# A gated linear recurrent unit moved from 128-row tiles to one 96-row weight block per tile, with its result brought back to 128 rows by DMA inside SBUF

## The chip, the core and the metric

The program runs on one core of one Trainium2 chip. The metric is the device time of one execution in microseconds (us); lower is better. The program before was timed three times: 2656.78, 2657.13 and 2657.72 us, median 2657.13 us. Engines are named as in the profile: PE (TensorE matmul), PEld (its weight load), DVE (VectorE), ACT (ScalarE), POOL (GpSimd), SP (SyncE, which here only issues the loads of the big weights).

## What is computed

Two transformer blocks run one after the other on one sequence of 256 tokens, width 2048, all in float32. The first block (gated linear attention, latent attention, SwiGLU) is not touched. The second block has two layers; each projects the normed input onto ten parts and mixes them by retention, differential attention and a linear recurrent unit of width 768. The change is in that last one, whose gates are block diagonal: 8 blocks of 96 columns.

```python
LRU_W, LRU_BLOCKS, LRU_BW = 768, 8, 96
def rg_lru(x, conv_w, conv_b, wa, ba, wx, bx, lam):
    xc = conv_b + xp[:, 0:S] * conv_w[0]          # causal convolution, 4 taps
    for j in range(1, CONV_W):
        xc = xc + xp[:, j:j + S] * conv_w[j]
    xb = xc.reshape(B, S, 8, 96)
    r = sigmoid(einsum('bsnk,nkj->bsnj', xb, wa) + ba)
    i = sigmoid(einsum('bsnk,nkj->bsnj', xb, wx) + bx)
    log_a = 8 * r * log_sigmoid(lam); a = exp(log_a)
    b = sqrt(-expm1(2 * log_a)) * (i * xc)
    h = scan over tokens of  h_t = a_t * h_(t-1) + b_t
lru_out = rg_lru(lx, ...) * silu(lg)              # part of the layer's mixed vector
y = concatenate([ret_out, diff_out, lru_out]) @ w_out
```

## The kernel before

**Units.** Every big product is a job, cut into units of 512 KB of weights. A unit's weights are loaded by SP into one of five `raw` slots. ACT rounds them into `whi` (the part that a fast float32r matmul takes exactly), DVE subtracts to get the rest, `wlo`, and PE multiplies: twelve matmuls of 512 columns a unit (or of 384 for the jobs `lx` and `lg`). `whi` and `wlo` have four slots. The order is fixed by `make_timeline`: before each unit n stands the preparation of unit n+3, and after each unit one step of each stage that is under way, such as the recurrent unit. All five engines run through that one list, each taking its own share and waiting on semaphores. So a stage's ACT and DVE work stands in the same queues as `whi` and `wlo`.

**Jobs around the recurrent unit.** In each layer of the second block the jobs are `rvg 0`, `lx 0`, `lx 1`, `rvg 1`, `dq`, `dk`, `dv`, `dg`, three `rqk`, `rvg 2`, `lg 0`, `lg 1` and four `w2`, each of eight units. The texts below call the units of `dq` dq1 to dq8 and those of `dk` dk1 to dk8. When `rvg 1` is done ACT evacuates it (`rv`, then `rg` with silu, which needs a table load before and leaves one behind).

**The recurrent unit, per layer and half (`hb` 0, 1).** PE transposes the projected columns into a PSUM bank per 128 rows (three banks `tp`, `lx_T`), ACT copies them to `LXT`. DVE runs the convolution, one `tensor_scalar` and three `scalar_tensor_tensor` per 128-row tile, a tile per step (`lx_conv`). The gates (`lru_g`, first for r, then for i) are plain float32 matmuls `tp<-xc,wa`: since 96 does not divide 128, a 128-row tile of the result needs the blocks of two or three tiles of the input, in all seven matmuls of 256 columns over three banks for 384 columns of a gate; the weights `WA` stand in 14 tiles of 128x128 which POOL first clears and then fills by 20 small DMAs (`ls_rn`). ACT applies the sigmoid per tile (`lxt<-tp,gcol`, `li<-tp,gcol`). `lru_a`: ACT exp and tanh per tile (`la<-lxt`, `lxt<-lxt`), DVE three elementwise operations over the half (768 columns). `lru_b`: ACT square root over the half (`xc<-xc`), DVE one product and a `tensor_tensor_scan` per tile. `lg_T`, some 200 us later, multiplies with silu of the gate and writes the tiles of `MXH` and `MXL`, the stationary operands of the last product.

The profile's `L825` is every matmul, `L828` every transpose, `L1260` every ACT function, `L1883`, `L1886`, `L1889` DVE's tensor_tensor, tensor_scalar and scalar_tensor_tensor, `L2331` the scan, `L2657` the DMAs of `WA`. The four TP banks are handed out in rotation, and a stage that writes a bank waits until its last reader is done (`empty`).

Of the kernel before, what the change touches and what calls it, by code (L numbers as in the profile page):

```python
# [16 lines left out]
P = 128  # L17
S = 256
# [119 lines left out]
NR1 = 94  # L138
R_CW, R_CB, R_BA, R_BX, R_LAM = 0, 48, 60, 72, 84
R_AB = 96  # L140
NR2 = 128
NRAW, NW = 5, 4
# [11 lines left out]
def lru_pieces():  # L154
    pieces, pairs = [], []
    for n in range(4):
        a0, a1 = 96 * n, 96 * n + 96
        cuts = [(max(a0, P * m), min(a1, P * m + P), m) for m in range(3) if max(a0, P * m) < min(a1, P * m + P)]
        for r0, r1, kt in cuts:
            for c0, c1, mt in cuts:  # L160
                if (kt, mt) not in pairs:
                    pairs.append((kt, mt))
                pieces.append((n, r0 - a0, r1 - a0, c0 - a0, c1 - a0, r0 - P * kt, c0 - P * mt, (kt, mt)))
    pairs.sort(key=lambda x: (x[1], x[0]))
    return pieces, pairs


PIECES, PAIRS = lru_pieces()
# [135 lines left out]
def stage_steps(sid):  # L304
# [64 lines left out]
    if kind == "lx":  # L369
        l, half = args  # L370
        return [idle, step(("lx_T", (l, half), 3))] + [step(("lx_conv", (l, 3 * half + m), 0)) for m in range(3)]
    if kind == "lru":
        (l,) = args
        return [x for hb in range(2) for x in (step(("lru_g", (l, hb, 0), 3)), step(("lru_g", (l, hb, 1), 3)), idle, step(("lru_a", (l, hb), 0)),
                                               step(("lru_b", (l, hb), 0)))]
# [194 lines left out]
def program(nc, ctx, I, CST, LVL, MSK, out):  # L570
# [3 lines left out]
    def sems(name, n):  # L574
# [11 lines left out]
    d_rowl, d_xr, d_gfb, d_gp, d_out = sem("d_rowl"), sems("d_xr", 2), sem("d_gfb"), sem("d_gp"), sem("d_out")  # L586

# [20 lines left out]
    lx_pad, xc_done, lru_exp, lru_tanh, lru_sum, lru_sqrt, scan_done, wa_zero = (  # L608
        sem(n) for n in ("lx_pad", "xc_done", "lru_exp", "lru_tanh", "lru_sum", "lru_sqrt", "scan_done", "wa_zero"))
# [46 lines left out]
    gcol = take("gcol", [224])  # L656
    modc = take("modc", [4, KD])
    cact = take("cact", [3, KD])
    clam = take("clam", [3, 12])
# [83 lines left out]
    LXT, XC, LA, LI = w2("lxt", 32, [6, 260]), w2("xc", 38.25, [6, S]), w2("la", 44.25, [3, S]), w2("li", 47.25, [3, S])  # L743
    DQT, DKT, DV, DG = w2("dqt", 32, [4, S]), [w2("dkt0", 44.25, [4, S]), w2("dkt1", 36, [2, S])], w2("dv", 48.25, [2, 512]), w2("dg", 52.25, [2, 512])
    WA = w2("wa", 56.25, [2, 14, P])
    RQK = w2("rqk", 56.25, [12, S])
    RAT = [w2("rat0", 68.25, [384]), w2("rat1", 90.25, [384])]
    DSX, DPT = [w2(f"dsx{i}", 91.75 + 1.5 * i, [384]) for i in range(2)], w2("dpt", 94.75, [384])
    RV, RG = w2("rv", 70.25, [2, 768]), w2("rg", 76.25, [2, 768])
    ST2 = [w2(f"st2{i}", 82.25 + 4 * i, [2, 512]) for i in range(2)]  # L750
# [70 lines left out]
    def pe_program(e):  # L821
# [38 lines left out]
        def rows(us):  # L860
            (u,) = us
            w.wait_ge(d_first, at("first"))
            bk = empty(u)
            tr(bk[:, 0:NR1], rows1[0:NR1, :], NR1)
            tr(bk[:, 128:128 + NR2], rows2[0:NR2, :], NR2).then_inc(tp_full[u.b], 1)

# [194 lines left out]
        def lx_T(us, l, half):  # L1061
            job = job_of["lx", l, half]
            w.wait_ge(gp_act[job["no"] % 2], at("gpa", *job["name"]))
            for m, u in enumerate(us):
                bk = empty(u)
                quad(bk, lambda a, t: ST2[job["st2"]][:, t, m * P:(m + 1) * P], 1).then_inc(tp_full[u.b], 1)

# [7 lines left out]
        def lru_g(us, l, hb, which):  # L1075
            m0 = 3 * hb
            w.wait_ge(wa_zero, l + 1)
            w.wait_ge(d_wa, 32 * len(PIECES) * (l + 1))
            for m in range(3):
                w.wait_ge(xc_done, at("xc", l, m0 + m))  # L1080
# [170 lines left out]
    def act_program(e):  # L1251
# [34 lines left out]
        def first_loads():  # L1286
            e.dma_start(cst[:, P:], CST[:, P:]).then_inc(d_first, 16)

            def rows(dst, r0, ap, n):
                e.dma_start(dst[r0:r0 + n, :], ap.rearrange("(r p) -> r p", p=P)).then_inc(d_first, 16)  # L1290
# [9 lines left out]
            rows(rows2, R_CW, I["lru_conv_w_2"].rearrange("l j d -> (l j d)"), 48)  # L1300
            rows(rows2, R_CB, I["lru_conv_b_2"].rearrange("l d -> (l d)"), 12)
            rows(rows2, R_BA, I["lru_ba_2"].rearrange("l d -> (l d)"), 12)
            rows(rows2, R_BX, I["lru_bx_2"].rearrange("l d -> (l d)"), 12)
            rows(rows2, R_LAM, I["lru_lambda_2"].rearrange("l d -> (l d)"), 12)
            rows(rows2, R_AB, I["ada_b"][0, 0:2 * D], 32)
# [19 lines left out]
        def rows(us):  # L1325
# [3 lines left out]
            copy(gcol[:, NR1:NR1 + NR2], bk[:, 128:128 + NR2]).then_inc(tp_act[u.b], 1)  # L1329
# [71 lines left out]
        def t_cexp(us):  # L1401
            gains()
            fn(clam[:, 0, :], gr(R_LAM, 12), ACT.Abs).then_inc(act_self, 1)
            w.wait_ge(act_self, own())
            fn(clam[:, 0, :], clam[:, 0, :], ACT.Exp, scale=-1.0).then_inc(act_self, 1)
            clam_exp[0] = own()

        def t_cln(us):
            w.wait_ge(act_self, clam_exp[0])
            fn(clam[:, 0, :], clam[:, 0, :], ACT.Ln, bias=unit_col).then_inc(clam_ln, 1)  # L1410
# [192 lines left out]
        def lx_T(us, l, half):  # L1603
            for m, u in enumerate(us):
                copy(LXT[:, 3 * half + m, 3:3 + S], full(u)[:, 0:S]).then_inc(tp_act[u.b], 1)
# [4 lines left out]
        def lru_g(us, l, hb, which):  # L1610
            m0 = 3 * hb
            gains()
            for m, u in enumerate(us):
                bk = full(u)
                dst = LXT[:, m0 + m, 0:S] if which == 0 else LI[:, m, :]
                if which == 1 and hb:
                    w.wait_ge(scan_done, at("scan", l, 0))
                fn(dst, bk[:, 0:S], ACT.Sigmoid, bias=gr((R_BX if which else R_BA) + 6 * l + m0 + m)).then_inc(tp_act[u.b], 1)
                note(tp_act[u.b], "tpa", *u)

        def lru_a(us, l, hb):
            m0 = 3 * hb
# [21 lines left out]
        def lg_T(us, l, half):  # L1644
            for m, u in enumerate(us):
                w.wait_ge(tp_dve[u.b], at("tpd", *u))
                copy(MXH[:, 10 + 3 * half + m, :], XC[:, 3 * half + m, :]).then_inc(mxg_hi, 1)
# [62 lines left out]
        def evac(us, no):  # L1710
# [167 lines left out]
    def dve_program(e):  # L1878
# [71 lines left out]
        def ada_mod(us, seq):  # L1950
# [4 lines left out]
            stt(scale, bk[:, 4:8], 1.0, gr(R_AB + KD + 4 * seq, 4), ALU.add, ALU.add).then_inc(dve_self, 1)  # L1955
            v = own()
            tt(shift, bk[:, 0:4], gr(R_AB + 4 * seq, 4), ALU.add).then_inc(tp_dve[u.b], 1)
# [80 lines left out]
        def t_cfin(us):  # L2038
            w.wait_ge(clam_ln, 1)
            gains()  # L2040
            stt(clam[:, 1, :], gr(R_LAM, 12), 0.0, clam[:, 0, :], ALU.min, ALU.subtract).then_inc(dve_self, 1)
            w.wait_ge(dve_self, own())
            ts(clam[:, 2, :], clam[:, 1, :], -8.0, None, ALU.mult).then_inc(clam_done, 1)
            ts(clam[:, 0, :], clam[:, 1, :], 8.0, None, ALU.mult).then_inc(clam_done, 1)
# [249 lines left out]
        def lx_T(us, l, half):  # L2294
# [452 lines left out]
```

## Time and profile before

| | |
|---|---|
| three timed runs | 2656.78, 2657.13, 2657.72 us (median 2657.13) |
| the profiled execution, span from the first to the last instruction | 2656.8 us |
| PE busy | 2569.4 us, 97% of the span |
| DVE, ACT, POOL busy | 1718.7 us (65%), 1303.5 us (49%), 76.9 us (3%) |
| mean granted TensorE clock | 0.996 |
| DMA traffic | 554.27 MB, mean 209 GB/s |

The page has no time of the profiled execution beyond its span, so the span is its own time here. A matmul in plain float32 stands in the trace as two records; the records are pipelined, so their single durations overlap and a group is read by its distance to the next. The view "chain" follows the work that ended last, piece by piece in order of time. The view "timeline" gives start, duration, engine, line, operation, tile and count, and in brackets the idle time before and what ended it.

### The profile page before, as it was taken

What the parts mean: (1) busy time and instruction counts of PE and PEld (TensorE: products, weight loads), DVE (VectorE), ACT (ScalarE), POOL (GpSimd) and SP (SyncE); (2) the same over time, 40 slices, a digit from 0 to 9 for tenths busy, and PEclk for the clock granted to TensorE, in tenths of its full rate; (3) what the DMA queues carried; (4) which work ended last, traced back from release to release, by engine and by line L of the source; (5) the groups of instructions that cost most, each with busy time, mean ns of one, the idle gap of its engine ahead of it and who ended that gap; (6) DMA issues with size and microseconds to landing.
All of it is one profiled execution on the core that took longest, in us unless ns stands there. A gap on an engine that the chain in (4) does not pass through costs nothing.

```text
span 2656.8 us, 35508 instructions
## 1 busy us (share of the span) xinstructions
PE 2569.4 (97%) x12983; PEld 2181.5 (82%) x12983; DVE 1718.7 (65%) x2262; ACT 1303.5 (49%) x1900; POOL 76.9 (3%) x116
## 2 busy tenths in 40 slices
PE   3989999999999999999999999999999999999999
PEld 3888887888887887888888888889888888888887
DVE  6877776776766756677655555566656655566664
ACT  3345455434555445444443444455654545565553
POOL 0000000000000000000000000002000101100000
PEclk9999999999999999999999999999999999999999
DMA  9975665887676765787666666566465465555564
GB/s 365 348 247 159 187 202 175 303 298 265 210 246 198 234 211 169 248 264 259 223 198 192 186 186 183 188 191 190 146 190 173 136 215 149 174 177 175 148 201 134
DMA packets 325063, 554.27 MB, mean 209 GB/s; under 512 B 24462, under 2 KB 135804, under 8 KB 324252
## 3 DMA queue, kind: packets, MB, share of 16 engines
q1 hardware_dynamic: 319104, 541.79, 64.1%
q0 software_dynamic: 3168, 7.12, 0.8%
q10 hardware_dynamic: 2620, 3.09, 0.3%
q8 instruction: 106, 1.74, 0.3%
q14 instruction: 65, 0.53, 0.1%
HBM read 549.83 MB, written 2.10 MB: 208 GB/s over the span
## 4 chain that ended last, share of the span: by engine, by line
PE 90%; DVE 4%; ACT 3%; issue 2%; DMA 1%; SPq 0%; POOL 0%; DVEq 0%; ACTq 0%
PE gp L825 82%; PE tp L825 5%; PE tp L828 2%; DMA raw_first<-in_ada_w_dram 1%; ACT whi L1260 1%; DVE wlo L1883 1%; DVE acc L1889 0%; ACT L1260 0%; DVE xs L1883 0%; ACT hraw L1260 0%; SPq L808 0%; DVE stat L2207 0%; ACT sx L1260 0%; DVE sx L1883 0%; DVE yd L1883 0%
## 5 line engine op out<-in xcount | busy, mean ns | idle before, releaser
L1883 DVE TENSOR_TENSOR wlo<-raw,whi 128x1024 fp32r<-128x1024 f32 (+1 forms) x830 | 983.2, 1197 | 641.0 <-ACT whi L1260 637.4
L1260 ACT ACTIVATE whi<-raw 128x1024 fp32r<-128x1024 f32 (+1 forms) x830 | 848.2, 1036 | 607.3 <-PE gp L825 483.6
L825 PE MATMUL gp<-whi,h 128*128 128x512 f32 (+1 forms) x2944 | 928.8, 387 | 6.1 <-DVE wlo L1883 4.6
L825 PEld LDWEIGHTS gp<-whi,h 128*128 128x128 f32 x2944 | 550.8, 188 | 107.6 <-issue 10.4
L825 PE MATMUL gp<-h,whi 128*128 128x512 f32 (+1 forms) x1936 | 605.5, 372 | 24.7 <-DVE wlo L1883 10.9
L825 PE MATMUL gp<-wlo,h 128*128 128x512 f32 (+1 forms) x1472 | 560.4, 381 | 0.0
L825 PE MATMUL gp<-h,wlo 128*128 128x256 f32 x1680 | 474.8, 283 | 0.0
L825 PEld LDWEIGHTS gp<-h,whi 128*128 128x128 f32 x1936 | 352.7, 192 | 96.4 <-issue 20.4
L825 PEld LDWEIGHTS gp<-h,wlo 128*128 128x128 f32 x1680 | 320.5, 191 | 0.8 <-issue 0.7
L825 PEld LDWEIGHTS gp<-wlo,h 128*128 128x128 f32 x1472 | 277.6, 189 | 45.2 <-issue 1.0
L1889 DVE SCALAR_TENSOR_TENSOR acc<-raw,cact,acc 128x1024 f32<-128x1024 f32 x149 | 190.5, 1278 | 7.4 <-DMA raw<-in_ada_w_dram 6.6
L825 PE MATMUL gp<-whi,ah 128*128 128x512 f32 x352 | 137.5, 391 | 0.0
L825 PE MATMUL gp<-whi,al 128*128 128x512 f32 x352 | 137.0, 389 | 0.0
L825 PE MATMUL gp<-wlo,ah 128*128 128x512 f32 x352 | 136.9, 389 | 0.0
L825 PE MATMUL gp<-whi,mxh 128*128 128x512 f32 x256 | 99.8, 390 | 0.0
L825 PE MATMUL gp<-whi,mxl 128*128 128x512 f32 x256 | 99.6, 389 | 0.0
L825 PE MATMUL gp<-wlo,mxh 128*128 128x512 f32 x256 | 99.6, 389 | 0.0
L825 PEld LDWEIGHTS gp<-whi,al 128*128 128x128 f32 x352 | 66.1, 188 | 13.9
L825 PEld LDWEIGHTS gp<-wlo,ah 128*128 128x128 f32 x352 | 66.1, 188 | 13.6
L825 PEld LDWEIGHTS gp<-whi,ah 128*128 128x128 f32 x352 | 66.1, 188 | 13.4
L2597 POOL TENSOR_TENSOR stat<-stat,cst 128x2 f32<-128x2 f32 (+1 forms) x37 | 30.1, 815 | 1467.6 <-DVE stat L1886 1467.5
L1260 ACT ACT_TABLE_LOAD x44 | 56.5, 1283 | 6.1 <-issue 2.8
(333 smaller groups left out, 2640.0 us busy)
## 6 DMA issues: line engine op xcount, KB each, us to landing
raw<-in_w_in_dram SPq DMA_DIRECT2D x310, 512.0 KB, 4.3
raw<-in_ffn_w_in_dram SPq DMA_DIRECT2D x176, 512.0 KB, 4.7
raw<-in_ada_w_dram SPq DMA_DIRECT2D x158, 512.0 KB, 5.0
raw<-in_w_out_dram SPq DMA_DIRECT2D x96, 512.0 KB, 4.3
raw<-in_ffn_w_down_dram SPq DMA_DIRECT2D x88, 512.0 KB, 4.3
raw<-in_w_in_dram SPq DMA_DIRECT2D x64, 384.0 KB, 3.5
raw_first<-in_ada_w_dram SPq DMA_DIRECT2D x34, 512.0 KB, 8.9
raw<-in_gla_wo_dram SPq DMA_DIRECT2D x32, 512.0 KB, 5.7
```

The costliest lines, as they stand in the source:

```text
L825: return e.matmul(o, l, r, start=start, stop=stop)
L828: return e.transpose(o, i, ident[0:n, 0:n])
L1260: return e.activation(o, i, f, **kw)
L1883: return e.tensor_tensor(o, a, b, op)
L1889: return e.scalar_tensor_tensor(out=o, in0=a, scalar=s, in1=b, op0=op0, op1=op1)
L2597: e.tensor_tensor(dst, dst, cst[:, C_HALF:C_HALF + n], ALU.pow).then_inc(pow_out, 1)
```

## The change

The recurrent unit works on 96 partitions, with one of the 8 weight blocks per tile. Per layer and half there are four tiles of 96 rows instead of three of 128.

- Transposes: eight of 96 columns into two banks instead of six of 128 into three. ACT copies two tiles of 96x2x256.
- Gates: four matmuls of a 96x96 block each instead of seven of 128x128, into two banks.
- Convolution, sigmoid, exp, tanh and scan run four times on 96 rows instead of three times on 128. The elementwise operations over a half have 1024 columns instead of 768.
- A half has one more convolution step, so the gates, `lru_a` and `lru_b` stand one unit later.
- `WA` is 96 rows by 8 blocks, filled by two DMAs a layer with no clearing.
- After the scan of each half POOL issues six DMAs from `XC` to `XG`, which has 128-row tiles. `lg_T`, the evacuation of `dg` and the rotation of `rqk` wait for them (`d_xg`).
- The small vectors are loaded in rows of 96, and the bias of the first block's modulation goes to the first of the two row tiles. Places in SBUF are dealt anew.

```diff
-PIECES, PAIRS = lru_pieces()
+    pieces = []
+    for b in range(4):
+        for m in range(3):
+            f0, f1 = max(BW * b, P * m), min(BW * b + BW, P * m + P)
+            if f0 < f1:
+                pieces.append((b, f0 - BW * b, f1 - BW * b, m, f0 - P * m))
...
-        return [idle, step(("lx_T", (l, half), 3))] + [step(("lx_conv", (l, 3 * half + m), 0)) for m in range(3)]
+        return [idle, step(("lx_T", (l, half), 2))] + [step(("lx_conv", (l, 4 * half + m), 0)) for m in range(4)]
...
     pe: lru_g
-            w.wait_ge(wa_zero, l + 1)
-            w.wait_ge(d_wa, 32 * len(PIECES) * (l + 1))
+            w.wait_ge(d_wa, 32 * (l + 1))
...
-                ks = [kt for kt, mt in PAIRS if mt == m]
-                for n, kt in enumerate(ks):
-                    last = mm(bk[:, 0:S], WA[:, which, 7 * hb + PAIRS.index((kt, m)), :], XC[:, m0 + kt, :], n == 0, n == len(ks) - 1)
+                for a in range(2):
+                    b = 4 * hb + 2 * m + a
+                    last = mm(bk[0:BW, a * S:(a + 1) * S], WA[0:BW, which, b, :], XC[0:BW, b, :], True, True)
...
     act: lru_a
-            for m in range(3):
-                ci = 6 * l + m0 + m
-                fn(LA[:, m, :], LXT[:, m0 + m, 0:S], ACT.Exp, scale=clam[:, 0, ci:ci + 1]).then_inc(lru_exp, 1)
+            for m in range(4):
+                ci = 8 * l + m0 + m
+                fn(LA[0:BW, m, :], LXT[0:BW, m0 + m, 0:S], ACT.Exp, scale=clam[0:BW, 0, ci:ci + 1]).then_inc(lru_exp, 1)
...
     act: evac
+                if kind == "dg":
+                    w.wait_ge(d_xg, 16 * len(PIECES) * (2 * args[0] + 2))
...
     dve: lru_b
-            for m in range(3):
-                e.tensor_tensor_scan(XC[:, 3 * hb + m, :], LA[:, m, :], LI[:, m, :], 0.0, ALU.mult, ALU.add).then_inc(scan_done, 1)
+            for m in range(4):
+                e.tensor_tensor_scan(XC[0:BW, 4 * hb + m, :], LA[0:BW, m, :], LI[0:BW, m, :], 0.0, ALU.mult, ALU.add).then_inc(scan_done, 1)
...
     dve: lg_T
-            w.wait_ge(scan_done, at("scan", l, half))
+            w.wait_ge(d_xg, 16 * len(PIECES) * (2 * l + half + 1))
...
     pool: ls_rn, lru_b
-            e.memset(WA[:, :, :, :], 0.0).then_inc(wa_zero, 1)
-            w.wait_ge(wa_zero, l + 1)
             for i, name in enumerate(("lru_wa_2", "lru_wx_2")):
-                for n, r0, r1, c0, c1, pr, pc, pair in PIECES:
-                    slot = PAIRS.index(pair)
-                    src = I[name][l, n:n + 5:4, r0:r1, c0:c1].rearrange("b r c -> r b c")
-                    e.dma_start(WA[pr:pr + r1 - r0, i, slot:slot + 8:7, pc:pc + c1 - c0], src).then_inc(d_wa, 16)
+                e.dma_start(WA[0:BW, i, :, :], I[name][l].rearrange("b r c -> r b c")).then_inc(d_wa, 16)
+
+        def lru_b(us, l, hb):
+            w.wait_ge(scan_done, at("scan", l, hb))
+            for b, r0, r1, m, p0 in PIECES:
+                e.dma_start(XG[p0:p0 + r1 - r0, 3 * hb + m, :], XC[r0:r1, 4 * hb + b, :]).then_inc(d_xg, 16)
```

ACT's queue in the first layer, from the gates of the first half to the exp and tanh of that half (`whi` is a unit's preparation, `rv` and `rg` the evacuation of `rvg 1`). Before:

```order
L1260 ACTIVATE lxt<-tp,gcol 128x256 x3
L1260 ACTIVATE whi<-raw 128x1024
L1260 ACTIVATE li<-tp,gcol 128x256 x3
L1260 ACTIVATE whi<-raw 128x1024 x2
L1260 ACTIVATE rv<-gp,stat 128x256 x2
L1260 ACT_TABLE_LOAD
L1260 ACTIVATE rg<-gp,stat 128x256 x2
L1260 ACT_TABLE_LOAD
L1260 ACTIVATE la<-lxt,clam 128x256 x3
L1260 ACTIVATE lxt<-lxt,clam 128x256 x3
```

The same place on ACT in the changed program:

```order
L1261 ACTIVATE lxt<-tp,gcol 96x256 x4
L1261 ACTIVATE whi<-raw 128x1024
L1261 ACTIVATE li<-tp,gcol 96x256 x4
L1261 ACTIVATE whi<-raw 128x1024
L1261 ACTIVATE rv<-gp,stat 128x256 x2
L1261 ACT_TABLE_LOAD
L1261 ACTIVATE rg<-gp,stat 128x256 x2
L1261 ACTIVATE whi<-raw 128x1024
L1261 ACT_TABLE_LOAD
L1261 ACTIVATE la<-lxt,clam 96x256 x4
L1261 ACTIVATE lxt<-lxt,clam 96x256 x4
```

One `whi` that stood ahead of the evacuation now stands between the evacuation and the exp.

DVE's queue in the first layer, from `lru_a` of the second half to the second rotation step of `dq` (`dqt` and the product with `cosv`). Before:

```order
L1889 SCALAR_TENSOR_TENSOR xc<-xc,lxt 128x768
L1883 TENSOR_TENSOR wlo<-raw,whi 128x1024
L1883 TENSOR_TENSOR li<-li,xc 128x768
L2331 SCALAR_TENSOR_TENSOR xc<-la,li 128x256 x3
L1883 TENSOR_TENSOR wlo<-raw,whi 128x1024 x2
L1883 TENSOR_TENSOR dqt<-st_166,sinv 128x8x32 x2
L1883 TENSOR_TENSOR st_166<-st_166,cosv 128x8x32 x2
L1883 TENSOR_TENSOR st_166<-st_166,dqt 128x8x32 x2
L1883 TENSOR_TENSOR wlo<-raw,whi 128x1024
L1883 TENSOR_TENSOR dqt<-st_166,sinv 128x8x32 x2
```

The same place on DVE in the changed program:

```order
L1895 SCALAR_TENSOR_TENSOR xc<-xc,lxt 96x1024
L1889 TENSOR_TENSOR wlo<-raw,whi 128x1024
L1889 TENSOR_TENSOR li<-li,xc 96x1024
L2339 SCALAR_TENSOR_TENSOR xc<-la,li 96x256 x4
L1889 TENSOR_TENSOR wlo<-raw,whi 128x1024
L1889 TENSOR_TENSOR dqt<-st_167,sinv 128x8x32 x2
L1889 TENSOR_TENSOR st_167<-st_167,cosv 128x8x32 x2
L1889 TENSOR_TENSOR st_167<-st_167,dqt 128x8x32 x2
L1889 TENSOR_TENSOR wlo<-raw,whi 128x1024
L1889 TENSOR_TENSOR dqt<-st_167,sinv 128x8x32 x2
```

Behind the scans of the second half one `wlo` stands ahead of the rotation instead of two; the other is now made ahead of them. The second layer has the same rows in the same places.

## Rows read from the trace of the kernel before

**Rows 1.** The page: busy time of each engine, and the chain by line.
```profile
PE 2569.4 (97%) x12983; PEld 2181.5 (82%) x12983; DVE 1718.7 (65%) x2262; ACT 1303.5 (49%) x1900; POOL 76.9 (3%) x116
...
PE gp L825 82%; PE tp L825 5%; PE tp L828 2%; DMA raw_first<-in_ada_w_dram 1%; ACT whi L1260 1%; DVE wlo L1883 1%; DVE acc L1889 0%; ACT L1260 0%; DVE xs L1883 0%; ACT hraw L1260 0%; SPq L808 0%; DVE stat L2207 0%; ACT sx L1260 0%; DVE sx L1883 0%; DVE yd L1883 0%
```

**Rows 2.** Instructions of tile xc: duration in ns min/median/max, first and last start.
```profile
L825 PE MATMUL tp<-xc,wa x112: 377/379/483, 1872.3 to 2327.7; 128*128 128x256 f32 x112
...
L1889 DVE SCALAR_TENSOR_TENSOR xc<-lxt,gcol,xc x36: 483/485/487, 1846.2 to 2297.8; 128x256 f32<-128x256 f32 x36
```

**Rows 3.** Chain of the first layer, 1780 to 1930 us: start, duration, what.
```profile
1875.51 2.75 PE gp L825 x12
1878.26 3.02 PE tp L825 x14
...
1902.05 24.50 PE gp L825 x108
1926.55 0.44 PE tp L828 x4
```

**Rows 4.** Timeline of PE in the first layer, the fourth group of gate matmuls.
```profile
1897.79 1.02 PE L825 MATMUL tp<-xc,wa 128*128 128x256 f32 x4
1899.62 2.43 PE L825 MATMUL tp<-xc,wa 128*128 128x256 f32 x10 [0.81 <-ACT lxt L1260]
```

**Rows 5.** Chain of the second layer, 2240 to 2370 us.
```profile
2304.26 3.02 PE tp L825 x14
...
2328.06 24.53 PE gp L825 x108
```

**Rows 6.** Timeline of ACT in the first layer, evacuation of rvg 1 to dq8.
```profile
1886.78 0.84 ACT L1260 ACTIVATE rv<-gp,stat 128x256 f32<-128x256 f32 x2 [1.60 <-PE gp L825]
...
1891.08 1.31 ACT L1260 ACTIVATE la<-lxt,clam 128x256 f32<-128x256 f32 x3
...
1893.63 1.04 ACT L1260 ACTIVATE whi<-raw 128x1024 fp32r<-128x1024 f32 x1
...
1895.99 0.85 ACT L1260 ACTIVATE xc<-xc 128x768 f32<-128x768 f32 x1
...
1900.18 1.06 ACT L1260 ACTIVATE whi<-raw 128x1024 fp32r<-128x1024 f32 x1
...
1904.88 1.06 ACT L1260 ACTIVATE whi<-raw 128x1024 fp32r<-128x1024 f32 x1 [1.37 <-PE gp L825]
```

**Rows 7.** Timeline of DVE in the first layer, lru_b of the second half and rotation.
```profile
1913.05 0.96 DVE L1883 TENSOR_TENSOR li<-li,xc 128x768 f32<-128x768 f32 x1 [0.86 <-ACT xc L1260]
1914.05 1.86 DVE L2331 TENSOR_TENSOR_SCAN xc<-la,li 128x256 f32<-128x256 f32 x3
1915.82 2.33 DVE L1883 TENSOR_TENSOR wlo<-raw,whi 128x1024 fp32r<-128x1024 f32 x2
1918.07 0.75 DVE L1883 TENSOR_TENSOR dqt<-st,sinv 128x256 f32<-128x256 f32 x2
...
1920.33 1.22 DVE L1883 TENSOR_TENSOR wlo<-raw,whi 128x1024 fp32r<-128x1024 f32 x1
```

**Rows 8.** Timeline of ACT: copies of the rotated tiles on 128 and 64 partitions.
```profile
1927.03 0.60 ACT L1260 ACTIVATE dqt<-tp 128x512 f32<-128x512 f32 x1 [2.05 <-PE tp L828]
...
1949.77 0.59 ACT L1260 ACTIVATE dkt<-tp 64x512 f32<-64x512 f32 x1 [2.04 <-PE tp L828]
```

**Rows 9.** Timeline of POOL: issue of the DMAs of one gate's weights.
```profile
1826.29 5.75 POOL L2657 DMA_DIRECT2D wa<-in_lru_wx_dram  x10
```

**Rows 10.** Timeline of DVE: preparations while POOL issues DMAs, and after.
```profile
1829.39 0.96 DVE L1883 TENSOR_TENSOR wlo<-raw,whi 128x768 fp32r<-128x768 f32 x1 [1.12 <-ACT whi L1260]
...
1835.63 0.96 DVE L1883 TENSOR_TENSOR wlo<-raw,whi 128x768 fp32r<-128x768 f32 x1 [1.12 <-ACT whi L1260]
```

**Rows 11.** Timeline of the start: transposes of the small vectors, first reader of them.
```profile
18.26 0.63 PE L828 MATMUL tp<-cst,rows 94*128 94x94 f32 x2 [11.35 <-DMA rows<-in_ada_b_dram]
...
30.32 0.17 DVE L1883 TENSOR_TENSOR cact<-gcol 128x16 f32<-128x16 f32 x1
```

More of the change, by code:

```diff
@@ L154, in lru_pieces @@
 def lru_pieces():
[L155 to L165, printed above, removed]
-PIECES, PAIRS = lru_pieces()
+    pieces = []
[4 more added lines that the diff above has]
+                pieces.append((b, f0 - BW * b, f1 - BW * b, m, f0 - P * m))
+    return pieces
+PIECES = lru_pieces()
 def make_jobs(I):
@@ L370, in stage_steps @@
         l, half = args
[L371 removed]
+        return [idle, step(("lx_T", (l, half), 2))] + [step(("lx_conv", (l, 4 * half + m), 0)) for m in range(4)]
     if kind == "lru":
         (l,) = args
[L374 removed]
+        return [x for hb in range(2) for x in (step(("lru_g", (l, hb, 0), 2)), step(("lru_g", (l, hb, 1), 2)), idle, step(("lru_a", (l, hb), 0)),
                                                step(("lru_b", (l, hb), 0)))]
@@ L1065, in lx_T @@
                 bk = empty(u)
-                quad(bk, lambda a, t: ST2[job["st2"]][:, t, m * P:(m + 1) * P], 1).then_inc(tp_full[u.b], 1)
+                for a in range(2):
+                    b = 2 * m + a
+                    for t in range(2):
+                        last = tr(bk[0:BW, (2 * a + t) * P:(2 * a + t + 1) * P], ST2[job["st2"]][:, t, b * BW:(b + 1) * BW])
+                last.then_inc(tp_full[u.b], 1)
         def lg_T(us, l, half):
@@ L1604, in lx_T @@
             for m, u in enumerate(us):
-                copy(LXT[:, 3 * half + m, 3:3 + S], full(u)[:, 0:S]).then_inc(tp_act[u.b], 1)
+                b = 4 * half + 2 * m
+                copy(LXT[0:BW, b:b + 2, 3:3 + S], tok_pairs(full(u)[0:BW, :])).then_inc(tp_act[u.b], 1)
                 note(tp_act[u.b], "tpa", *u)
@@ L1610, in lru_g @@
         def lru_g(us, l, hb, which):
-            m0 = 3 * hb
             gains()
@@ L1614, in lru_g @@
                 bk = full(u)
-                dst = LXT[:, m0 + m, 0:S] if which == 0 else LI[:, m, :]
                 if which == 1 and hb:
                     w.wait_ge(scan_done, at("scan", l, 0))
-                fn(dst, bk[:, 0:S], ACT.Sigmoid, bias=gr((R_BX if which else R_BA) + 6 * l + m0 + m)).then_inc(tp_act[u.b], 1)
+                for a in range(2):
+                    n = 2 * m + a
+                    b = 4 * hb + n
+                    dst = LXT[0:BW, b, 0:S] if which == 0 else LI[0:BW, n, :]
+                    fn(dst, bk[0:BW, a * S:(a + 1) * S], ACT.Sigmoid, bias=gr((R_BX if which else R_BA) + 8 * l + b)).then_inc(tp_act[u.b], 1)
                 note(tp_act[u.b], "tpa", *u)
         def lru_a(us, l, hb):
-            m0 = 3 * hb
+            m0 = 4 * hb
             w.wait_ge(clam_done, 2)
@@ L1646, in lg_T @@
                 w.wait_ge(tp_dve[u.b], at("tpd", *u))
-                copy(MXH[:, 10 + 3 * half + m, :], XC[:, 3 * half + m, :]).then_inc(mxg_hi, 1)
+                copy(MXH[:, 10 + 3 * half + m, :], XG[:, 3 * half + m, :]).then_inc(mxg_hi, 1)
         def rp_T(us, kind, l, j, k):
@@ L2355, in rp_r @@
             w.wait_ge(scan_done, at("scan", l, 1))
+            if kind == "rqk":
+                w.wait_ge(d_xg, 16 * len(PIECES) * (2 * l + 2))
             rope_ready()
```

114 lines of the change are left out of this document (59 added, 55 removed).

## The prediction

> **What bounds the kernel now.** I read the page first. PE is busy for 97% of the span, and 82% of the chain is the big matmuls [rows 1]: where PE has no gap, work taken from it shortens the run, and work added to ACT or DVE costs nothing. The change does both, so the question is how much ACT and DVE have to spare exactly where it acts. The instructions of `xc` give the kinds and counts: 112 records of the gates, two per matmul, so 56 matmuls, in eight groups of seven [rows 2]. The chain around the recurrent unit shows the groups in PE's row: 3.02 us a group, 0.216 a record, and 24.50 us for nine units of twelve matmuls, 2.72 a unit [rows 3]. Between the third and the fourth group the chain does not run through PE. PE's timeline shows why: the fourth group stops because its banks are still held by the sigmoids of the third, and it takes 4.26 us (1897.79 to 1902.05) instead of 3.02, a stall of 1.24 [rows 4]. The second layer repeats this: from the start of the second group to the end of the fourth it is 23.80 us there, 23.79 here [rows 3, 5]. So what I work out for one layer counts twice. Last come the timelines of ACT and DVE [rows 6, 7]. ACT is occupied without a pause from 1886.78 until it waits 1.37 us ahead of 1904.88, and then again. The recurrent unit already takes nearly all that ACT can give in this stretch, although ACT is busy for only 49% of the run.
>
> **PE.** A group becomes four matmuls of the same 256 columns: 8 x 0.216 = 1.73 us, 1.29 less. What 96 rows and columns do to the time of a matmul no row shows. If it fell in proportion, a group would take 1.30; if a group took as long as seven do now, 3.02. I take 0.216 a record, the row of the same moving columns. A transpose takes 0.11 us (0.44 for four [rows 3]); two more per half make 0.44 a layer. By PE alone a layer then loses 4 x 1.29 - 0.44 = 4.7 us, and the bank stall of 1.24 goes too: r and i take two of the four banks each, so i no longer waits for r. That makes 6.0 a layer.
>
> The Trainium skill ("TensorE: Matmul & The Clock Gate", the table under why this matters) says that a lone matmul of small K takes as long as one with K of 128. By that rule the sum stands as it is; by proportion to 96 rows it would end 1.7 us lower. No run here shows it yet.
>
> **ACT and DVE.** Time here goes by elements per partition: the copy of 512 columns takes 0.59 us on 64 partitions and 0.60 on 128 [rows 8], so four operations on 96 rows cost four thirds of three on 128. ACT gets two sigmoids, one exp and one tanh more per half at some 0.4 each, and 0.2 on the square root: 1.8 us. DVE gets a convolution tile of 1.9 (three of 0.485 [rows 2] and a tensor_scalar that I put at the same), 0.27 on each of four products, and a scan of 0.6: 3.6 us.
>
> The convolution is hidden. In the narrow units of `lx 1`, three quarters of 2.72 or 2.04 us each, a step costs DVE 1.9 and a preparation of 0.96 [rows 10], 0.8 more than PE takes. Four such steps put it 3.3 us behind; preparations stand three units, 6.1 us, ahead.
>
> **The stretch where it is not hidden.** I follow the first layer, unit by unit, in the new order (exp and tanh come one preparation later; before the rotation of `dq` one `wlo` stands instead of two).
>
> PE ends `rvg 1` at 1886.76 now. Two groups (2.58) less and the transposes (0.44) more put that at 1884.6.
>
> ACT from there, each step a distance of [rows 6]:
> - `rv` to exp 4.30 (1886.78 to 1891.08), plus the `whi` that now stands between, 1.05: exp at 1889.95.
> - eight functions instead of six, 2.55 + 0.82 = 3.37 (the row of three is 1.31, so 0.41 for one more): `whi` of dq5 at 1893.3.
> - 2.36 to the square root: 1895.7. From it to the `whi` of dq7 4.19, plus 0.2 and 0.4: 1900.5.
> - from there ACT needed 3.33 until it was idle (1904.88 - 1.37 - 1900.18), in which its last sigmoid waited for PE's group that ended at 1902.05. That wait is gone and about pays for the fourth sigmoid; I take 3.4: `whi` of dk1 at 1903.9, with no idle time left.
> - second half: 2.36, 3.37, 2.36 and the square root itself, 1.06: its end at 1913.0.
>
> DVE from there [rows 7]: its product starts at 1913.05, where it starts today. Product 1.00 + 0.27, scans to `wlo` 1.77 + 0.59: the `wlo` of dk3 runs from 1916.7 to 1917.9. Then half the rotation (2.26), the `wlo` of dk4 ready at 1921.3, the other half, the `wlo` of dk5 ready at 1924.7.
>
> PE meanwhile: from 1884.6 ten units and two groups, 27.2 + 3.46, so it wants dk3 at 1915.3. It waits 2.6 us for it, 0.7 for dk4 (1921.3), does the four transposes and starts dk5 at 1924.7. Now it starts dk5 at 1926.99 (1926.55 + 0.44 [rows 3]). So a layer gains 2.3 us, not 6.0: 3.7 of it is given back as new waits on `wlo`. Behind dk5 DVE has caught up and PE leads again, so the 2.3 stay.
>
> **The rest.** The transfer to `XG` follows the scan by at most the 4 or so us of six short DMAs (ten issues took POOL 5.75 [rows 9]), and its first waiters, `dg` and `rqk`, come more than two jobs of 22 us later: nothing. Ten issues a gate and a clearing become two: POOL is not waited for there, nothing. The small vectors are transposed at 18.26, and DVE first reads them at 30.32 [rows 11]; a slightly different layout does not use up 12 us.
>
> **Sum.** 2656.8 - 2 x 2.3 = 2652.2 us of span. The median of the runs stands 0.3 over the profiled span, so 2652.5.
>
> **Rivals.**
> - *PE alone decides.* If ACT and DVE keep up, all 6.0 a layer come: 2657.1 - 12.0 = 2645.1. For it: PE's 97%, the idle 65% and 49% of the others over the run. Against it: the local rows, where ACT has 1.37 us of idle time in 18 and gets 3.6 more work by dk3.
> - *The new waits take everything.* If the path through ACT is 2 us longer than my distances say (a preparation that is late for another reason, such as its `raw` slot), the gain is 0 to 0.5 a layer: 2656 to 2657.2. Also here: if a 96-row group should cost the full 3.02.
> - *POOL holds DVE up: slower.* The six DMAs behind the last scan are issued exactly while DVE works off `wlo` and rotation, on which PE waits. Six issues take 3.45 us [rows 9]. If DVE stood still for all of it, a layer would lose 3.45 - 2.3 = 1.15: 2659.4. It turns slower when the hold is over 2.3 of the 3.45 us. Against it: a `wlo`, with two operands in SBUF, took 0.96 us while POOL issued DMAs and 0.96 after [rows 10]. The Trainium skill ("GPSIMD Engine Reference", Specifications) says that GpSimd's SBUF access contends with DVE instructions that have two SBUF inputs; all of these have. By that rule this rival comes true; the trace of before speaks against it.
>
> **How the numbers follow.** Forecast 0.64, the first rival 0.13, the second 0.14, the slower one 0.06, others 0.03. What a measurement can tell from no change is 0.2%, 5.3 us, so faster means below 2651.8. The forecast's own range is 2650.5 (groups in proportion to 96 rows, 1.7 lower) to 2654.5 (2 us from four passages of distances that could each be 0.5 off); a third of it is under 2651.8. With the first rival: 0.37 faster. Slower by over 5.3 us needs more than a full hold: 0.05. The rest, 0.58, is within. The range runs from 2647.0, leaving out the full gain of PE, to 2656.5, leaving out the slower rival and the end of the second.
>
> **What would show it.** Right: gate groups of 1.73 us; no stall inside the fourth group; no idle ACT between `rv` and the second square root; PE waiting 2 to 3 us on `wlo` at dk3 and again under 1 us at dk4, in both layers; dk5 some 2.3 us earlier against the start of `lx 1`. Wrong: no wait there (first rival); waits of 5 us or more, or `wlo` rows over 1.3 us beside POOL's issues (third).

## The result and the profile after

The changed kernel takes 2668.01 us (median of 4 runs, 2666.99 to 2673.36), the kernel before 2657.43 (2656.78 to 2658.32): a ratio of 1.0043, 95% interval 1.0031 to 1.0056. The forecast was 2652.5 with a range up to 2656.5. The change made the kernel slower by 11 us where I had it 5 us faster. The profiled execution took 2666.99 us, with a span of 2665.2. In what follows e1 to e12 are the twelve experiments, in their order.

The page after, busy time of each engine [rows 1]:
```profile
span 2665.2 us, 35450 instructions
...
PE 2574.2 (97%) x12943; PEld 2171.0 (81%) x12943; DVE 1731.4 (65%) x2282; ACT 1309.7 (49%) x1912; POOL 63.1 (2%) x102
```
PE has 40 instructions less than before (48 records of the gates less, 8 transposes more) and is busy for 4.8 us more. That already says that something other than the recurrent unit has changed.

The instructions of tile `xc` after [rows 2], duration min/median/max:
```profile
L824 PE MATMUL tp<-xc,wa x64: 377/379/379, 1884.0 to 2333.1; 96*96 96x256 f32 x64
...
L1895 DVE SCALAR_TENSOR_TENSOR xc<-lxt,gcol,xc x48: 479/481/483, 1855.1 to 2309.9; 96x256 f32<-96x256 f32 x48
L2668 POOL DMA_DIRECT2D xg<-xc x24: 501/522/547, 1909.2 to 2353.9; - x24
...
L2339 DVE TENSOR_TENSOR_SCAN xc<-la,li x16: 659/663/689, 1906.4 to 2350.4; 96x256 f32<-96x256 f32 x16
```
The chain of the first layer, start, duration, what [rows 3]:
```profile
1884.15 1.73 PE tp L824 x8
1885.88 2.75 PE gp L824 x12
1888.62 1.73 PE tp L824 x8
1890.35 2.76 PE gp L824 x12
...
1929.73 3.01 PE gp L824 x12
1932.74 0.44 PE tp L827 x4
```
PE's timeline there, from the third gate group to dk3, a wait in brackets [rows 4], and then DVE's [rows 7]:
```profile
1901.09 1.89 PE L824 MATMUL tp<-xc,wa 96*96 96x256 f32 x8
...
1905.57 1.89 PE L824 MATMUL tp<-xc,wa 96*96 96x256 f32 x8
...
1926.33 0.47 PE L824 MATMUL gp<-whi,h 128*128 128x512 f32 x1 [2.33 <-ACT whi L1261]
```
```profile
1921.38 1.22 DVE L1889 TENSOR_TENSOR li<-li,xc 96x1024 f32<-96x1024 f32 x1 [0.89 <-ACT xc L1261]
1922.64 2.43 DVE L2339 TENSOR_TENSOR_SCAN xc<-la,li 96x256 f32<-96x256 f32 x4
1924.99 1.20 DVE L1889 TENSOR_TENSOR wlo<-raw,whi 128x1024 fp32r<-128x1024 f32 x1
```
All of this is as predicted: groups of 1.73 us, none of them interrupted, and a new wait of 2.33 us at dk3. The view names ACT's `whi` for that wait, but the `whi` of dk3 had ended at 1922.30; what dk3 waited for is its `wlo`, which DVE ran from 1924.99 to 1926.19, behind the scans, as forecast.

Where the time went shows when both traces are laid side by side. Each of the 858 `whi` preparations stands at the same place in both programs, so the start of the k-th one after, less that before, is how far the changed kernel lags:

| `whi` no. | start before, us | lag, us | what lies between |
|---|---|---|---|
| 48 | 214.3 | -0.99 | start |
| 288 | 986.6 | +3.40 | first block, mixers |
| 432 | 1405.4 | +4.62 | the same, and `dn 0` |
| 480 | 1538.8 | +6.07 | `dn 0` |
| 528 | 1674.5 | +6.07 | feed-forward, from `h` |
| 576 | 1810.7 | +8.53 | `dn 1` |
| 624 | 1946.7 | +6.37 | recurrent unit, layer 1 |
| 672 | 2098.1 | +6.35 | attention parts |
| 720 | 2235.9 | +8.52 | `w2`, layer 1 |
| 768 | 2372.7 | +6.35 | recurrent unit, layer 2 |
| 857 | 2632.7 | +8.20 | `w2`, layer 2 |

The two recurrent units gain 2.2 us each, against the 2.3 forecast. The loss lies in stretches in which the change edits nothing. The chain there has unbroken runs of 96 big matmuls, in `dn 1` before and after:
```profile
1750.88 21.80 PE gp L825 x96
```
```profile
1758.28 22.33 PE gp L824 x96
```
Before, 227.1 ns from one to the next; after, 232.6. The stationary operand is `ah` or `al`. Taken pair by pair from the starts in the trace, the distance grows wherever the stationary operand lies in the work region: by 5 to 6 ns for `ah`, `al`, `mxh`, `mxl`, `ogh` and `ogl`, by less for some of the smaller ones (under 3 ns for the latents of the first block), 15.9 us together over 3125 distances. It does not grow where the stationary operand lies in `h` (1472 of `whi,h` to `wlo,h`: 227 and 227).

The change widened `gcol` from 224 to 256 columns. That moves everything placed behind it, `acc`, `brow` and the work region, by 128 bytes, while `WHI`, `WLO` and `H2`, ahead of it, stay. Before, the moving operands (`WHI`, `WLO`) and the work region both started at 128 above a multiple of 256 bytes; now the work region starts at 0 above one, and the moving operands still at 128.

### The profile page after: what moved, and what is told of

Read it like the earlier page. It is cut to its first block, busy times and chain, and to the rows that moved or that the text cites. A ratio compares the mean times of both kernels' runs of the same rounds, so it can differ in the third digit from the quotient of the medians.

```text
span 2665.2 us, 35450 instructions
## 1 busy us (share of the span) xinstructions
PE 2574.2 (97%) x12943; PEld 2171.0 (81%) x12943; DVE 1731.4 (65%) x2282; ACT 1309.7 (49%) x1912; POOL 63.1 (2%) x102
## 4 chain that ended last, share of the span: by engine, by line
PE 87%; DVE 5%; ACT 4%; issue 2%; DMA 1%; SPq 0%; POOL 0%; DVEq 0%; ACTq 0%
PE gp L824 80%; PE tp L824 5%; PE tp L827 2%; ACT whi L1261 1%; DVE wlo L1889 1%; DMA raw_first<-in_ada_w_dram 1%; DVE acc L1895 1%; ACT L1261 1%; ACT hraw L1261 0%; SPq L807 0%; ACT lxt L1261 0%; ACT la L1261 0%; DVE stat L2213 0%; ACT sx L1261 0%; DVE xs L1889 0%
```

## Experiments

**1 to 3: put the place back, take it alone, move everything.** One number for each of e1 and e2, two for e3; `stat` has unused columns at its end, so making it smaller moves what lies behind it and nothing else.
```
e1:  changed kernel   stat = take("stat", [800])     # -128 bytes
e2:  kernel before    stat = take("stat", [736])     # -384 bytes
e3:  changed kernel   stat = take("stat", [800]); base = ... + 128
```


> The changed kernel with one number changed: the area of small vectors between the table cst and the work region is given 128 bytes less (the spare end of stat), so that acc, brow and the whole work region lie at the addresses they have in the kernel before. Placement theory (the 11 us come from where the stationary operands start in SBUF): the distance between two big matmuls on ah, mxh and ogh falls from 232 to 227 ns, all drift outside the recurrent unit goes, and the run takes 2657.4 - 2 x 2.2 = 2653 us, 15 below the changed kernel and 4 below the one before. Rival (the recurrent unit's own edits, its transfers or its changed loads cost the 11 us, and the longer distance has another cause): 2667 to 2669, distances still 232.

> The kernel before with nothing changed but the place: the area of small vectors is given 384 bytes less, so acc, brow and the work region start at 256 instead of 128 bytes above a multiple of 512, as they do in the changed kernel. Placement theory: the distances on ah, mxh, ogh rise from 227 to 232 ns, 2657.4 + 15 = 2672 us (2669 to 2674). Rival (the place costs nothing): 2656.5 to 2658.5, distances 227.

> As the first of these three, but everything in SBUF lies 128 bytes higher: the stationary operands of the work region are at 256 above a multiple of 512 as in the changed kernel, and the moving operand (whi, wlo) is now at 256 too, so stationary and moving start alike again. If what counts is that the two start alike: 2653 us, 227 ns everywhere. If what counts is where the stationary operand itself starts: 232 ns on ah, mxh and now on h too, which was at 227 ns so far; some 4400 more matmuls at 5 ns, so about 2653 + 15 + 22 = 2690 us. If what counts is where the moving one starts: also 232 everywhere.

Measured: e1 2655.42 us, ratio to the kernel before 0.9992 (0.9983 to 1.0000), span 2652.2; e2 2674.81, 1.0063 (1.0049 to 1.0076), span 2673.1; e3 2653.46, 0.9988 (0.9979 to 0.9997), span 2654.7. The runs of 96 matmuls in the chains of e1, e2 and e3:
```profile
1776.25 21.83 PE gp L824 x96
```
```profile
1760.74 22.33 PE gp L825 x96
```
```profile
1751.47 21.80 PE gp L824 x96
```
The place alone, without the recurrent unit's change, costs the kernel before 17 us, more than the changed kernel lost (I had expected 2669 to 2674 us); and put back, the loss is gone. What is left of a gain is small: e1 is 1.9 us under the kernel before in the median, with an interval that ends at no change, where I had expected 4. One reason is below, behind experiments 7 and 8. e3 settles what about the place counts: both operands are where they were never before, and it is fast. It is not where the stationary operand starts but whether the two start alike.

**4: the matmul by itself, in 64 pairs of places.**
```
for rs in RES: for rm in RES: for i in range(24):
    matmul(bank, st[rs][:, i % 4, :], mv[rm])   # 128x128, 128x512 float32r
```


> Leaves out the whole computation: after 48 matmuls of lead it does 24 matmuls of the big kind (128 stationary columns, 512 moving, float32r) for each of 64 pairs of places, the stationary operand starting at 0, 64, ..., 448 bytes above a multiple of 512 and the moving one likewise; no DMA, ACT or DVE runs beside them. Placement theory in its plain form: 227 ns where both start at 128, 232 where the stationary one starts at 256 and the moving one at 128, and the table tells whether the rest goes by the stationary place or by the pair. Rival (the distance grows only through what other engines do to the same memory at that moment): one value, 227 or less, in all 64 places.

Measured, mean distance in ns between starts, stationary operand at 128 bytes; the other seven rows have the same values moved along:

| moving operand at | 0 | 64 | 128 | 192 | 256 | 320 | 384 | 448 |
|---|---|---|---|---|---|---|---|---|
| ns | 233.1 | 233.5 | 228.5 | 229.0 | 232.4 | 233.3 | 227.3 | 229.0 |

So it goes by the difference, moving less stationary, modulo 256: 227.2 at 0, 229.0 at 64, 232.4 at 128, 233.3 at 192, to 1.3 ns, with neither DMA nor ACT nor DVE at work. The rival of this experiment (others' traffic) is out. It is one execution, with 24 matmuls for each pair of places.

**5, 6: the table carried back to the kernel.** `stat` of 784 and 816 columns.

> The changed kernel with acc, brow and the work region 64 bytes lower than in the kernel before (192 lower than in the changed one), so that the moving operand starts 64 bytes above the stationary one, modulo 256. The table of places gives 229.0 instead of 227.2 ns there. Place theory: 1.8 ns x some 3100 matmuls = 5.6 us over the version without the shift (span 2652.2): span 2657.8, and a median 5 to 6 above that version's. Rival (any displacement costs the same 5 ns, a matter of alike or not alike): 15 us, 2667.

> The same, 64 bytes higher than in the kernel before: the moving operand now starts 64 below the stationary one, which is 192 above it modulo 256, and the table gives 233.3 ns. Place theory: 6.1 ns x 3100 = 18.9 us over the version without the shift: span 2671, the slowest placement of all, although the shift is as small as in the last one. Rival (only the size of the displacement counts): as the last one, 2658.

Chains of e5 and e6:
```profile
1754.01 22.00 PE gp L824 x96
```
```profile
1755.71 25.20 PE gp L824 x108
```
229.2 and 233.3 ns, as in the table, although the displacement is the same size. The affected distances add up to 5.4 and 18.4 us against 5.6 and 18.9 expected. Spans 2659.1 and 2665.6, medians 2659.29 (ratio 1.0003, 0.9994 to 1.0012) and 2667.48 (1.0033, 1.0021 to 1.0045). e5's span is 1.3 over and e6's 5.4 under what I expected; what experiment 9 found explains most of that. The medians, each as a ratio to the kernel before measured beside it, rise by less than the profiles: e5 by 0.0011 over e1 (2.9 us, 5.6 expected) and e6 by 0.0041 (10.9 us, 18.9 expected).

**7, 8: what limits the recurrent unit.** Old place in both. e7 works on three quarters of the columns on ACT and DVE; e8 computes the sigmoids by tanh. That removes three table loads a layer, and gives exp and tanh a bias operand that they did not have.
```
e7:  ... LXT[0:BW, b, 0:Q], LI[0:BW, n, 0:Q], LA[0:BW, m, 0:Q], XC[..., 0:Q]   # Q = 192
e8:  fn(dst, bk[...], ACT.Tanh, scale=0.5, bias=...)        # biases halved once
     stt(li, li, 1.0, x3, ALU.add, ALU.mult)                # 2 i x
     fn(x3, x3, ACT.Sqrt, scale=0.25)                       # the 1/2 put back
     fn(LA, LXT, ACT.Exp, scale=c/2, bias=c/2)              # and the tanh likewise
```


> The changed kernel in the old place, where ACT and DVE work on 192 of the 256 columns from the sigmoids to the scan (a quarter of that work is left out; the convolution, PE's work and the transfers are whole). Theory (the recurrent unit gained 2.2 us a layer and not 6.0 since ACT and DVE decide there): the chain's ACT pieces shrink by a quarter of their column part (32 functions a layer at 0.43 go to about 0.34, the root from 1.06 to 0.8: 3.4 us), so each layer gives 3 to 3.6 us more, the span is 2652.2 - 6.6 = 2645.6 and PE waits for wlo at dk3 by less than 0.5 us. Rival (PE's own work, or a preparation late for its raw slot, decides): under 1 us a layer, 2650.5 or more.

> The changed kernel in the old place, its sigmoids computed as (1 + tanh(z/2))/2, so that gates, exp and tanh use one set of tables: one ACT_TABLE_LOAD of 1.28 us a layer is gone from the chain of the stretch (ahead of the exp of the second half; the one ahead of the first gates lies in ACT's idle time). Theory (ACT decides there): 1.2 to 1.3 us a layer, span 2652.2 - 2.6 = 2649.6, which would be 7 below the kernel before. Rival (DVE's products, scans and wlo decide, ACT only seems to): 0 to 0.3 a layer, 2652.

e7: 2650.04 us, ratio 0.9965 (0.9951 to 0.9978), span 2647.9 where 2645.6 was expected. Its units gain 4.6 us each against the kernel before. That is 2.4 to 2.5 more than those of the changed kernel, less than the 3 to 3.6 I expected, and 3.2 more than those of e1. In PE's timeline the wait at dk3 is gone; the one at dk4, which was 0.41 in the changed kernel, is left:
```profile
1918.18 0.47 PE L825 MATMUL gp<-whi,h 128*128 128x512 f32 x1 [0.43 <-DVE wlo L1890]
```
So what e7 gave back is that one wait of 2.33 us; the one at dk4 stands behind the rotation, which e7 leaves whole. The rival (under 1 us a layer) is out.

e8: 2652.16 us, ratio 0.9975 (0.9965 to 0.9985), span 2649.7 where 2649.6 was expected. Its units gain 3.5 us each against the kernel before, 1.3 more than those of the changed kernel, and PE's wait at dk3 is 1.19 us instead of 2.33. The number is as expected, but it is a sum that I had not seen. ACT has 38 table loads instead of 44, three a layer less. One lies in idle time; two lie where ACT is the limit, ahead of `rg` and ahead of the exp of the second half. ACT's timeline in e1 and then in e8:
```profile
1881.61 0.84 ACT L1261 ACTIVATE rv<-gp,stat 128x256 f32<-128x256 f32 x2 [0.96 <-PE gp L824]
1882.47 1.28 ACT L1261 ACT_TABLE_LOAD   x1
1883.76 0.84 ACT L1261 ACTIVATE rg<-gp,stat 128x256 f32<-128x256 f32 x2
...
1901.76 1.28 ACT L1261 ACT_TABLE_LOAD   x1
1903.05 1.71 ACT L1261 ACTIVATE la<-lxt,clam 96x256 f32<-96x256 f32 x4
```
```profile
1884.59 0.84 ACT L1261 ACTIVATE rv<-gp,stat 128x256 f32<-128x256 f32 x2 [0.96 <-PE gp L824]
1885.32 0.84 ACT L1261 ACTIVATE rg<-gp,stat 128x256 f32<-128x256 f32 x2
...
1903.92 2.10 ACT L1261 ACTIVATE la<-lxt,clam 96x256 f32<-96x256 f32 x4
```
Without the load, `rg` starts 0.73 us behind `rv` instead of 2.15, so a load is worth 1.4 us here, and two of them 2.8. Against that, four exps or tanhs with the bias take 2.1 us instead of 1.71, four times a layer: 1.5 us. The difference is the 1.3. That the expected 1.3 (one load and nothing else) came out is luck; that ACT's path decides is shown by both experiments, and it was the reason for 2.3 and not 6.0 in the forecast.

**Why e1 gained less than the changed kernel in its units.** The units of e1 gain 1.45 us each, those of the changed kernel 2.16, and the edit and the wait of 2.33 us at dk3 are the same. The granted clock is not. It is 1.00 in the unit dk3 of the changed kernel and 0.50 (1.2 GHz instead of 2.4) in that of e1, in windows of e1 and then of the changed kernel (us, busy of PE, PEld, DVE, ACT, POOL, granted clock, DMA share, GB/s):
```profile
1915.00:1918.00 3.00, 3.00 (x8) 2.33 (x8) 2.93 (x8) 0.00 (x0) 1.88 (x4) 0.50 0.79 214
```
```profile
1926.40:1929.00 2.60, 2.60 (x12) 2.08 (x12) 2.53 (x7) 0.00 (x0) 2.01 (x4) 1.00 0.74 167
```
It costs 0.7 us where it happens: the slower unit takes the place of the wait at dk4. In the profiles it happened behind 6 of the 12 waits of 2.3 us (both layers of e1 and e6, the second of e3 and e5, none of the changed kernel and e11), and behind none of the 6 shorter ones of e7, e8 and e12. What chooses is not shown. It explains 0.7 of the 3.2 by which e7's units are ahead of e1's.

**9: other widths, and the pairs of 512 and 256 columns.** While laying these traces side by side I met a second thing. In the units with `h` as moving operand, 1385 pairs of a 512- and a 256-column matmul, a pair takes 346.7 or 353.3 ns for the same work, for tens of us at a time, and each execution has another mix (488.2 us together in the profile before, 486.0 after, 485.7 in e1, 482.0 in e6).
```
burst(st, mv[r], [512, 256], 49)      # four places, four beginnings each
burst(st, mv[0], [512, 256, 256, 512], 48)
```


> Leaves out the whole computation, as the first table does. The moving operand starts 0, 32, ..., 224 bytes above a multiple of 256, the stationary one at 0: 24 matmuls each for 512, 384 and 256 columns in float32r and 512 in bf16; then 512 and 256 columns in turn, as the units with h as moving operand do it, at four places and from four different beginnings each, and at last in the order 512, 256, 256, 512. Place theory: at 512 columns the values of the first table return at every second place (227, 229, 232, 233) and the odd ones lie between; at 256 and 384 columns a like number of ns per matmul, not in proportion to the columns. For 512 and 256 in turn, the traces so far show two steady values for the same work, 346.7 and 353.3 ns a pair, that hold for tens of us and then change: if that hangs on the beginning, both appear here at place 0; if it needs what the other engines do, one only. Rival to the place theory as a general one: at 256 columns or in bf16 nothing changes with the place.

| mean ns, moving less stationary | 0 | 32 | 64 | 96 | 128 | 160 | 192 | 224 |
|---|---|---|---|---|---|---|---|---|
| 512 columns | 226.7 | 233.3 | 228.8 | 233.9 | 233.3 | 234.3 | 233.3 | 233.3 |
| 384 columns | 173.3 | 173.3 | 173.3 | 176.7 | 176.0 | 176.7 | 174.7 | 174.0 |
| 256 columns | 119.4 | 117.8 | 117.8 | 119.7 | 118.7 | 117.3 | 113.3 | 118.2 |
| 512, bf16 | 215.8 | 215.8 | 215.8 | 215.8 | 215.8 | 215.8 | 215.8 | 215.8 |

The rule holds for 512 columns in float32r. I had expected like amounts at 256 and 384: wrong, 384 loses at most 3.4 ns and 256 is best at 192. In bf16 the place does nothing. The pairs in turn at place 0 took 346.6 ns from three beginnings and 353.5 from another (eight short matmuls ahead of them, where the others had six, seven or nine): two steady rhythms, and the beginning chooses. At 64 bytes there are two as well (348.9 and 353.3), at 128 and 192 one (351.1 and 353.3). In the order 512, 256, 256, 512 it was 348.1 to 348.3 from all four. All of it is one execution.

**10 to 12: both found costs taken out of both kernels.**
```
if i % 2 and 0 < nth < K - 1:      # every second block of columns
    mm(o[:, 0:S], wl[:, kk, fs], hh, False, False)
    last = mm(o, wh[:, kk, fs], H2[:, k, :, :]..., False, False)
    continue
```


> The kernel before with one edit in PE's program: in the units with h as moving operand every second block of columns does its 256-column matmul ahead of its 512-column one, so that the order is 512, 256, 256, 512 instead of 512, 256 in turn; same work. The second table gives 348.3 ns a pair for that order from all four beginnings, where turns give 346.7 or 353.3. Theory of the two steady values: the 1385 pairs take 482.4 us instead of the 488.2 of the profile before, span 2656.8 - 5.8 = 2651, and the runs lie closer together. Rival (the two values come from the other engines' traffic, which this does not touch): 2657, with stretches of 353 still there.

> The changed kernel in the old place with the same edit of the order. Both kernels are now free of what the place and the two steady values add, so that this against the last one is the change itself: by the forecast 2 x 2.2 = 4.4 us less, span 2646.6. Rival (the 2 us between the medians of the changed kernel in the old place and the kernel before are all that there is): 2649.

> The changed kernel in the old place, gates by tanh, and the same edit of the order: another 2 x 1.3 us less, span 2644.0, some 0.45% under the kernel before and the best of all. Rival: 2647 or more, if with the pairs in order the stretch of the recurrent unit is bound otherwise.

| | median (runs), us | span | ratio to the kernel before |
|---|---|---|---|
| e10, before, order | 2653.29 (2651.95 to 2654.53) | 2652.3 | 0.9983 (0.9974 to 0.9992) |
| e11, changed, old place, order | 2652.27 (2649.85 to 2653.31) | 2648.6 | 0.9979 (0.9970 to 0.9988) |
| e12, with gates by tanh too | 2647.18 (2645.71 to 2648.02) | 2643.9 | 0.9961 (0.9949 to 0.9974) |

In the feed-forward a unit with `h` as moving operand takes 2.793 us in all three profiles; it was 2.826 in the kernel before and 2.773 in e6. e10 took 4.5 us off where 5.8 were expected, and not all of it is the order: its start is 1.3 us later, the stretches with `h` as moving operand (`whi` 240 to 528) give 4.3, and 1.5 come from the granted clock behind the norm between the two layers (below). The runs of e10 lie within 2.6 us (11 runs), those of the kernel before beside them within 6.0 (21 runs).

With the rhythm gone, the lag of e11 behind e10 is flat to 0.13 us from `whi` 240 to the first unit and to 0.03 between it and the end of that layer, and falls by 2.16 in the first unit and 2.16 in the second. That of e12 falls by 3.49 and 3.55, and e12 is the best version found, 0.4% under the kernel before. e11 came out 2 us over my 2646.6: one part is this, in PE's windows of the first unit behind the norm, at the end of the first layer, in e11 and e12 (columns as above):
```profile
2219.00:2222.00 3.00, 3.00 (x11) 2.39 (x10) 2.04 (x4) 0.83 (x1) 0.00 (x0) 0.69 0.00 0
```
```profile
2216.00:2219.00 3.00, 3.00 (x14) 2.44 (x15) 2.88 (x5) 1.94 (x5) 0.00 (x0) 1.00 0.00 0
```
Behind the 6 us or so in which PE waits there for the norm, with four transposes between, the mean granted clock was 0.69 in one (a part of the window at 1.2 GHz, a part at 2.4) and 1.00 in the other, and the first unit took 4.39 us instead of 3.01. The lag of e11 rises by 1.4 us there. So e11's span, 2648.6, lies nearer to the rival's 2649 than to my 2646.6, although both units gave the 2.2 that the rival denies. And e12's 2643.9 is my 2644.0 by luck: of the 4.7 us under e11 only 2.7 are its units', 1.4 are this clock and 0.8 lie at the start. The first unit behind the norm took 4.4 to 5.5 us in every profile in which the chain shows it by itself, those before and after the change among them, except e10 (2.99) and e12 (3.01). What chooses stays open.

The medians of e10 and e11 differ by only 1.0 us, where the units give 4.3. The mean granted clock of the runs goes with that: it is 0.996 in all eleven runs of e10, and in e11 0.996 in three (2649.85 to 2651.33 us), 0.995 in one and 0.994 in seven (2650.56 to 2653.31). In the kernel before it is 0.995 or 0.996. In e12, whose wait at dk3 is 1.2 us, it is 0.996 in all five. So the new wait of 2.3 us seems to cost more in most runs than in the profiled ones; only the profiled runs have a trace, so where the clock fell in the others is not shown.

## Why the prediction was wrong

The step that failed is one the prediction never gave a term: the layout. Under "The rest" it priced transfers, clearing and small vectors at nothing. Of the layout it asked only whether the small vectors are read in time ("a slightly different layout does not use up 12 us"), and not what else the wider `gcol` moves. Its cost is 15.9 us of longer distances. The balance of the two profiled executions closes: +15.9 of place, -4.3 of the two units, -1.0 at the start, -2.2 of the rhythm of the pairs make +8.4, and the spans are 8.4 apart. Undone (e1) and done alone (e2), it accounts for the whole turn to slower.

A second term is missing as well, a small one: "so the 2.3 stay" leaves out what the new wait at dk3 does to the clock. Behind half of these waits in the profiles the granted clock fell to 0.50, at 0.7 us a layer, which is a part of why e1 is 1.9 us under the kernel before in the median and not 4. By e1 the forecast for the stretch alone, 2652.5, would have been 2.9 us too low.

The rest of the working, step by step:
- *Gate groups of 1.73 us, 0.216 a record on 96 rows*: right; 377/379 ns, as on 128 rows, so not in proportion. The rule of the Trainium skill ("TensorE: Matmul & The Clock Gate") agrees with the trace here.
- *The stall inside the fourth group goes*: right, both later groups are unbroken runs of eight records.
- *PE waits 2.6 at dk3, 0.7 at dk4*: 2.33 and 0.41. *dk5 2.3 us earlier*: 2.16 in both layers (1.45 in e1, where the clock fell behind the wait).
- *ACT and DVE give back 3.7 of 6.0*: right in mechanism and size (3.8); e7 removed a quarter of their work and had 2.4 to 2.5 of it back, the whole wait at dk3. The chain runs through ACT from `rv` to the second square root, and from there through DVE's product, scans, `wlo` and rotation. I had priced ACT's work by distances and not noticed that six table loads of 1.28 us lie in that path; e8 took two of them out.
- *`XG` is late for nobody; POOL holds nobody up*: right. Six issues took 3.11 us and landed in 1.7 to 5.1. The scans had ended when they began; the `wlo` beside them kept their length (1.20 to 1.23 us each, as elsewhere), so the slower rival's mechanism did not act. The run was slower by another cause. POOL's timeline and DVE's:
```profile
1909.17 3.11 POOL L2668 DMA_DIRECT2D xg<-xc  x6 [81.94 <-DVE xc L2339]
```
```profile
1906.44 2.43 DVE L2339 TENSOR_TENSOR_SCAN xc<-la,li 96x256 f32<-96x256 f32 x4
1908.80 2.45 DVE L1889 TENSOR_TENSOR wlo<-raw,whi 128x1024 fp32r<-128x1024 f32 x2
```
- *Scans to `wlo` 1.77 + 0.59, product 1.00 + 0.27*: 2.35 and 1.26, from start to start; the tensor_scalar, put at 0.485, took 0.40.
- *The median 0.3 over the profiled span*: not a like comparison. In every later run the time is 1.8 us over its own span.
- *Small vectors*: the transposes moved from 18.26 to 19.11, and the first reader on DVE, at 31.18, did not wait.

The rivals all argued about the stretch that the diff edits. None asked what a shift of 128 bytes does to 3125 matmuls outside it, where 5 ns each, 2%, outweigh all that the unit gave. The working on that stretch held to within 0.3 us; it was the smaller part of what the diff did.

## What to carry to other kernels

When a diff changes the size of any buffer, list what is placed behind it and whether the operands of float32r matmuls of 512 columns among it keep their distance from the other operand modulo 256 bytes; pad so that they do. Where the effect of a change is a few us, lay the same instruction of both traces side by side over the whole run before explaining anything: it shows in one column which stretches changed, and the edited one may be innocent. A stretch bound by ACT is shortened by grouping functions by table set, which no busy share shows; count all the loads that go and what the new form of the functions costs. And a new wait of PE can cost more than its length, so look at the granted clock behind it.

## What was not expected of the hardware

- A float32r matmul of 128 stationary and 512 moving columns, with a new stationary operand each time, follows its predecessor after 227.2, 229.0, 232.4 or 233.3 ns, by the difference of the operands' starts modulo 256 bytes (0, 64, 128, 192), with all other engines idle; at odd multiples of 32 it is 233.3 to 234.3. In bf16 it is 215.8 everywhere. Why was not tried.
- Matmuls of 512 and 256 columns in turn have two steady rhythms, 346.7 and 353.3 ns a pair (a cycle of three pairs of 361, 349 and 350 ns in the slower one). With all else idle the beginning chose between them, in one execution; the order 512, 256, 256, 512 has one, 348.3. Over 1385 pairs that is up to 9 us. It is a part of the spread of this kernel's runs, 2.6 us instead of 6.0 in e10; how large a part is open, since the clock differs too.
- Behind the same wait of PE its granted clock fell to 0.50 in some executions and not in others: behind 2.3 us of waiting in 6 of 12 cases, for 0.7 us each; behind the norm in most profiles, for 1.4 us in e11.
- A table load of 1.28 us delayed the next function by 1.4 us (`rv` to `rg`, 2.15 with it and 0.73 without). Exp and tanh on 96x256 went from 1.71 to 2.1 us for four when they got a bias operand.
